# Small experts of an MoE stage in fp32 on two column halves of TensorE, with groups of three kinds

## Chip, core and metric

The kernel runs on one NeuronCore of a Trainium2 chip. The metric is the device time of one execution in microseconds, as the median of several runs.

## What is computed

One inference step of a layer for 1024 prompt rows and 8 streams of 16 rows, 1152 rows of width 2048: a mixer (short convolution and differential attention), then a hierarchical mixture of experts, then a final norm. What matters here is the mixture:

```python
lg = hf @ w_rg + b_rg;  g = argmax(lg)             # 4 groups of experts
le = (hf @ w_re + b_re)[its group];  top 2 of 8    # two experts per row
gu = ragged_dot(xs, w_ei, sizes)                   # 2048 -> 2 x 512, rows sorted by expert
gate, up = split(gu)
ys = ragged_dot(silu(gate) * up, w_eo, sizes)      # 512 -> 2048
y[tok] += ys * weight
```

Everything is fp32. The routing depends on the inputs. Worked out from the reference, the 2304 row-expert pairs of the given inputs fall on the 32 experts in this way:

93, 74, 55, 185, 49, 149, 43, 88, 22, 15, 12, 18, 13, 28, 27, 11, 44, 16, 29, 205, 118, 23, 86, 17, 68, 190, 228, 61, 34, 179, 14, 110.

## The kernel before

Only the expert stage (`phase_experts`) is touched. A group is up to 256 rows of one expert. Every expert here fits in one group, so groups 0 to 31 are the experts in the order above. A group has one tile of 128 rows or two ("a pair", over 128 rows).

**Weights.** An expert's 12.6 MB come as 12 units of 1 MB: 8 units of `w_ei` (256 of 2048 input rows, all 1024 columns) and 4 units of `w_eo` (512 output columns). SP loads them in order into a ring of RAW = 6 buffers (`load_unit`, L1492); it waits on `lo_done` of a buffer before it overwrites it. ScalarE rounds a unit to fp32r in `w_hi` (`split_hi`, L1891), VectorE subtracts to get `w_lo` (`split_lo`, L1979) and thereby frees the raw buffer. `w_hi` and `w_lo` have four slots each; TensorE frees a slot through `used`. So the splits run up to four units ahead of TensorE and the loads six ahead of the splits. The last things ScalarE and VectorE do in a group are the first four splits of the next one.

**Rows.** POOL gathers a group's rows by an indirect DMA per tile (`gather_tile`, L1640), the second tile only for a pair. TensorE transposes them (L1736) a quad of four 128x128 blocks at a time, ScalarE copies a quad to `xT_hi` (L1896) and VectorE makes `xT_lo` (L1984). The first tile of the next group is turned between this group's up and out products. The second tile of a next pair is turned (L1859, L1951, L2140) between `up_and_first` and `out_rest` of this group, under `pe.If(nx < nx2)`; VectorE does this ahead of its last two `split_lo` of the group.

**Products.** Each product is three fp32r matmuls: hi x hi, hi x lo, lo x hi. Up (L1805): 16 blocks of 128 input rows, two halves of 512 columns (256 gate and 256 up), 96 matmuls a tile. Out (L1782): 4 blocks of k, 4 units, 48 matmuls a tile. Between them: silu on ScalarE (L1928), multiply on VectorE (L2117), two transposes a half (L1769), and the hi and lo parts of the activation (L1933, L2122). The two halves let one be activated while TensorE works on the other. ScalarE evicts y (L1965) with the routing weight as scale; POOL scatters the tile's rows to `expert_rows` (L1711).

**Planning.** Ahead of the stage VectorE computes the place of each row, the expert of each group and how many groups before it are pairs. Engines read these as register values (`value_load`, L1564 and L1574). The loop runs 40 times on each engine, with `If(g < count)` around its body, and `by_size` picks a one-tile or two-tile body. POOL writes a table of rows by slot to memory and reads it back into `e_table` (L1691, L1692).

After the last group `phase_final` adds the two expert rows of each token to x and normalizes.

## Time and profile before

| | us |
|---|---|
| median of 3 runs | 3590.74 (3588.39 to 3593.21) |
| the profiled execution, its own time | 3590.53 |
| its span | 3588.5 |
| busy in the span: TensorE matmul / weight load | 3366.8 / 2950.7 |
| busy: VectorE / ScalarE / GpSimd | 1683.9 / 1288.3 / 1021.6 |
| mean granted clock of TensorE | 0.971 of full speed |

All times in the views are microseconds from the start of the span unless marked ns. PE is TensorE's matmuls, PEld its weight loads, DVE VectorE, ACT ScalarE, POOL GpSimd, SP the engine that issues most DMAs. Matmuls are pipelined, so the duration of one is longer than the distance to the next. A true fp32 matmul is listed as two records, an fp32r one as one. "Idle before, releaser" is the engine's idle time ahead of a group of instructions and what ended most of it; "issue" there is time in which it waited for nothing that the profile shows. The granted clock is 1.00 at TensorE's upper level (2.4 GHz) and 0.50 at its lower one (1.2 GHz).

### The profile page before, as it was taken

To read this page: it belongs to the slowest core of one execution; us is meant where nothing else is said; L and a number is where in the kernel's file an instruction comes from. 1 tells how busy PE (TensorE), PEld (TensorE's weight loads), DVE (VectorE), ACT (ScalarE), POOL (GpSimd) and SP (SyncE) were. 2 spreads that over 40 slices of the span, in tenths; PEclk is the share of its full clock that TensorE was granted. 3 is DMA by queue.
4 is the path that set the end of the run, shared out by engine and by line. 5 is a ranking of instruction groups with operands and counts; after the bars stand their busy time and mean duration, and the time that the engine had idled before them with its cause. 6 is when DMAs were issued, how large, how long until landed. Compare 5 with 4: busy or idle time off the path is not lost. (4 is left out here: it accounts for less than half of the span.)

```text
span 3588.5 us, 51245 instructions
## 1 busy us (share of the span) xinstructions
PE 3366.8 (94%) x18439; PEld 2950.7 (82%) x18440; DVE 1683.9 (47%) x1742; ACT 1288.3 (36%) x1577; POOL 1021.6 (28%) x761
## 2 busy tenths in 40 slices
PE   8999999999999998989999869999999999999990
PEld 8999999999999975668888657787888788778770
DVE  4222222000111147860111267658888858846677
ACT  4000000000000035750101246657787757746572
POOL 3444444444444301234445431101111101101010
PEclk9999999999999998999999879999999999999995
DMA  4121111212222391116445469679999979967688
GB/s 150 60 67 54 54 54 58 76 61 75 87 80 67 124 348 61 54 42 238 156 124 164 152 216 356 244 258 354 364 353 369 360 253 369 370 218 268 255 336 361
DMA packets 341083, 691.62 MB, mean 193 GB/s; under 512 B 23034, under 2 KB 151482, under 8 KB 330511
## 3 DMA queue, kind: packets, MB, share of 16 engines
q1 hardware_dynamic: 291508, 585.75, 45.9%
q10 hardware_dynamic: 37163, 66.14, 4.9%
q0 software_dynamic: 12336, 38.69, 3.1%
q8 instruction: 51, 0.84, 0.1%
q14 instruction: 25, 0.20, 0.0%
HBM read 637.25 MB, written 97.28 MB: 205 GB/s over the span
## 5 line engine op out<-in xcount | busy, mean ns | idle before, releaser
L1979 DVE TENSOR_TENSOR e_w_lo<-expert_raw,e_w_hi 128x2048 fp32r<-128x2048 f32 x388 | 872.8, 2288 | 255.1 <-ACT e_w_hi L1891 231.9
L1891 ACT ACTIVATE e_w_hi<-expert_raw 128x2048 fp32r<-128x2048 f32 x388 | 744.3, 1919 | 301.9 <-PE e_gu L1805 253.3
L295 PE MATMUL p_z<-hT_hi,p_w_hi 128*128 128x384 f32 x2256 | 755.3, 335 | 2.4 <-DVE p_xs L432 2.4
L297 PE MATMUL p_z<-hT_hi,p_w_lo 128*128 128x384 f32 x2256 | 753.8, 334 | 0.0
L296 PE MATMUL p_z<-hT_lo,p_w_hi 128*128 128x384 f32 x2256 | 753.7, 334 | 0.0
L295 PEld LDWEIGHTS p_z<-hT_hi,p_w_hi 128*128 128x128 f32 x2256 | 423.6, 188 | 2.7 <-DVE p_xs L432 2.7
L296 PEld LDWEIGHTS p_z<-hT_lo,p_w_hi 128*128 128x128 f32 x2256 | 423.6, 188 | 0.0
L297 PEld LDWEIGHTS p_z<-hT_hi,p_w_lo 128*128 128x128 f32 x2256 | 423.5, 188 | 0.0
L1805 PE MATMUL e_gu<-e_w_hi,e_xT_hi 128*128 128x512 f32 x1216 | 390.4, 392 | 6.6 <-issue 6.6
L1805 PE MATMUL e_gu<-e_w_lo,e_xT_hi 128*128 128x512 f32 x1216 | 387.8, 390 | 0.0
L1805 PE MATMUL e_gu<-e_w_hi,e_xT_lo 128*128 128x512 f32 x1216 | 387.8, 390 | 0.0
L277 POOL TENSOR_TENSOR p_w_raw<-p_w_raw,gain 128x1024 f32<-128x1024 f32 x96 | 182.2, 1898 | 668.8 <-issue 332.6
L1805 PEld LDWEIGHTS e_gu<-e_w_hi,e_xT_hi 128*128 128x128 f32 x1216 | 227.1, 188 | 60.7 <-issue 14.6
L1805 PEld LDWEIGHTS e_gu<-e_w_lo,e_xT_hi 128*128 128x128 f32 x1216 | 228.8, 188 | 48.1
L1805 PEld LDWEIGHTS e_gu<-e_w_hi,e_xT_lo 128*128 128x128 f32 x1216 | 228.8, 188 | 47.9
L1645 POOL COPY e_gather_idx<-e_table 128x2 int32 (+1 forms) x33 | 6.7, 204 | 879.9 <-PE e_t L1736 690.6
L283 POOL TENSOR_TENSOR p_w_lo<-p_w_raw,p_w_hi 128x1024 fp32r<-128x1024 f32 x96 | 237.7, 2476 | 7.7
L626 ACT ACTIVATE d_kT<-p_t 128x512 f32<-128x512 f32 x8 | 4.4, 596 | 613.0 <-DVE p_rows L496 602.3
L1782 PE MATMUL e_y_ps<-e_w_hi,e_aT_hi 128*128 128x512 f32 x608 | 199.9, 410 | 14.8 <-DVE e_w_lo L1979 6.9
L534 ACT ACTIVATE p_e_hi<-p_e 128x1152 fp32r<-128x1152 f32 x8 | 9.3, 1168 | 568.9 <-DVEq L476 568.9
L1429 DVE TENSOR_TENSOR m_x<-m_z,m_x 128x512 f32<-128x512 f32 x36 | 24.6, 692 | 373.1 <-PE m_z L2308 372.7
L1782 PE MATMUL e_y_ps<-e_w_lo,e_aT_hi 128*128 128x512 f32 x608 | 192.6, 398 | 0.0
(337 smaller groups left out, 4642.4 us busy)
## 6 DMA issues: line engine op xcount, KB each, us to landing
expert_raw<-w_ei SPq DMA_DIRECT2D x256, 1024.0 KB, 8.6
expert_raw<-w_eo SPq DMA_DIRECT2D x128, 1024.0 KB, 10.4
p_w_raw<-w_in SPq DMA_DIRECT2D x96, 512.0 KB, 4.0
m_w_raw<-w_out SPq DMA_DIRECT2D x64, 512.0 KB, 4.4
d_k<-cache_k SPq DMA_DIRECT2D x8, 2048.0 KB, 14.6
d_v<-cache_v SPq DMA_DIRECT2D x8, 2048.0 KB, 9.9
rows_back<-expert_rows SPq DMA_DIRECT2D x12, 1024.0 KB, 15.8
n_x<-x SPq DMA_DIRECT2D x9, 1024.0 KB, 5.9
```

Source lines behind the costliest of these rows:

```text
L277: pool.tensor_tensor(w_raw[:, part, :], w_raw[:, part, :], c.gain[:, part].unsqueeze(2).to_broadcast([P, HALF, P]), ALU.mult).then_inc(ste ...
L283: pool.tensor_tensor(w_lo[:, part, :], w_raw[:, part, :], w_hi[:, part, :], ALU.subtract).then_inc(split[half], 1)
L295: pe.matmul(out, w_hi[:, k, :], x_hi[:, xk, cols], start=(k == 0), stop=False)
L296: pe.matmul(out, w_hi[:, k, :], x_lo[:, xk, cols], start=False, stop=False)
L297: mm = pe.matmul(out, w_lo[:, k, :], x_hi[:, xk, cols], start=False, stop=(k == KT - 1))
L534: act.activation(e_hi[:], e[:], ACT.Copy).then_inc(hi_ready, 1)
L1429: dve.tensor_tensor(x[:, s, :], z[:, s, :], x[:, s, :], ALU.add).then_inc(x1_ready, 1)
L1645: pool.tensor_copy(gather_idx[:], field(g, 0)).then_inc(idx_ready, 1)
L1782: mm = pe.matmul(y_ps[:, m % 2, :], a_part[:, r, k, :], w_part[:, s, k * 512:(k + 1) * 512], start=(k == 0 and a_part is aT_hi and w_part ...
L1805: return pe.matmul(gu_ps[:, 2 * r + h, :].rearrange("p (b n) -> p b n", b=2), x_part[:, r, k, :], w[:, :, h, :], start=(k == 0 and x_part ...
L1891: act.activation(w_hi[:, s, :], raw[:, r, :], ACT.Copy).then_inc(hi_done, 1)
L1979: dve.tensor_tensor(w_lo[:, s, :], raw[:, r, :], w_hi[:, s, :], ALU.subtract).then_inc(lo_done[r], 1)
```

## The change

Groups get three kinds, SMALL (at most 64 rows), FULL (up to 128) and PAIR. The planner writes a third table `group_kind`, and each engine branches on it.

A SMALL group multiplies in true fp32 straight from the raw weights: no `split_hi`, no `split_lo`; the raw buffer is freed by the matmul itself. Its rows are held exactly in a new tile `xT` of 64 columns, so a matmul uses half the columns of the array, and the two halves of the output columns run on the two column halves, to PSUM partitions 0 to 63 and 64 to 127. The activation sits on 128 partitions and is done in one piece. Two units of `w_eo` are used at once, which is why they are loaded in the order 0, 2, 1, 3. y lies in halves of 1024 columns on the two partition halves and is scattered as 128 half rows; for this the row table gets two more fields and a copy `twice` doubled over the partition halves.

In other groups the products are as before. The second tile of a pair is now turned at the start of its own group, ahead of the up products, and the first unit is multiplied with the first tile alone before the second tile is awaited. POOL always gathers two tiles. TensorE and ScalarE no longer skip the loop's body behind the last group but branch three times in it.

```diff
+BLOCK_OF = (0, 2, 1, 3)
+FEW = P // 2
+SMALL, FULL, PAIR = 1, 2, 3
+FIELDS = 6
...
-        def by_size(eng, before, after, part):
-
-            with eng.If(before < after):
-                part(2)
-            with eng.If(before == after):
-                part(1)
+        def by_kind(eng, g, part):
+
+            kind = kind_of(eng, g)
+            for k in (SMALL, FULL, PAIR):
+                with eng.If(kind == k):
+                    part(k)
...
-                    gather_tile(0)
-                    with pool.If(before < after):
-                        gather_tile(1)
+                    for r in range(2):
+                        gather_tile(r)
...
+                first_tiles = io.slots.rearrange("(g p) f -> p g f", p=GROUP)[0:FEW, :, :]
+                for h in range(2):
+                    pool.dma_start(twice[h * FEW:(h + 1) * FEW, :, :], first_tiles[:, :, 2:FIELDS]).then_inc(twice_loaded, 16)
...
@@ tensor: up_and_first, start
-                        pe.wait_ge(x_kept, 4 * (g + here + n))
+                        pe.wait_ge(x_kept, 4 * (g + here + 1))
+                        pe.wait_ge(x_exact, 4 * (g + 1))
                         pe.wait_ge(a_kept, 2 * (g + here) + 1)
+                        if n == 2:
+                            turn_second()
...
+                            if u == 0:
+                                for r in range(n):
+                                    if r == 1:
+                                        pe.wait_ge(x_kept, 4 * tile)
+                                    for a in range(2):
+                                        for x_part, w_part in PASSES:
+                                            for h in range(2):
+                                                mm = product(u, a, r, x_part, w_part, h)
...
+                    def up_small():
...
+                        for u in range(UIN):
+                            pe.wait_ge(raw_loaded[u % RAW], 32 * g + 16 * (u // RAW) + 16)
+                            for a in range(2):
+                                k = 2 * u + a
+                                w = raw[:, u % RAW, a * 1024:(a + 1) * 1024].rearrange("p (b h n) -> p b h n", b=2, h=2)
+                                for h in range(2):
+                                    mm = pe.matmul(bank[side(h)], xT[:, k, :], w[:, :, h, :], start=(k == 0), stop=(k == KT - 1))
...
+                            mm.then_inc(lo_done[u % RAW], 1)
+
+                    def turn_act_small():
+                        pe.wait_ge(act_ready, 2 * (g + here) + 2)
+                        for j in range(2):
+                            mm = pe.transpose(gu_ps[:, 0, j * P:(j + 1) * P], act_rows[:, 0, j * P:(j + 1) * P], c.ident[:])
+                        mm.then_inc(a_turned, 2)
+
+                    def out_small(i):
+
+                        units = [UIN + 2 * i + h for h in range(2)]
...
+                        for k in range(KE):
+                            for h, u in enumerate(units):
+                                mm = pe.matmul(y_ps[side(h), i, :], aT[:, k % 2, side(k // 2)], raw[:, u % RAW, k * 512:(k + 1) * 512],
+                                               start=(k == 0), stop=(k == KE - 1))
...
+                    def group(kind):
+                        if kind == SMALL:
+                            up_small()
+                            pe.wait_ge(x_loaded, 32 * (g + 2))
+                            turn_rows(g + 1, g + here + 1, 0, (0,))
+                            turn_act_small()
+                            turn_rows(g + 1, g + here + 1, 0, (1, 2, 3))
+                            for i in range(UOUT // 2):
+                                out_small(i)
+                        else:
+                            up_and_first(tiles_of(kind))
+                            out_rest(tiles_of(kind))
+
+                    by_kind(pe, g, group)
...
@@ scalar
+                    def keep_small(split):
+                        for i in range(UOUT // 2):
+                            for h in range(2):
+                                product_done(UIN + 2 * i + h)
+                            c.hold(act)
+                            act.activation(y[:, 0, i * 512:(i + 1) * 512], y_ps[:, i, :], ACT.Copy,
+                                           scale=column_twice(g, 0)).then_inc(y_kept, 2)
+                            if split:
+                                for h in range(2):
+                                    split_hi(g + 1, 2 * i + h)
+
+                    def group(kind):
+                        n = tiles_of(kind)
+                        if kind == PAIR:
+                            for q in range(4):
+                                act.wait_ge(x_turned, 4 * (g + here + 1) + q + 1)
+                                act.activation(quad(xT_hi, 1, q), second_bank(q).rearrange("p (a b) -> p a b", a=4), ACT.Copy).then_inc(x_hi, 1)
+                        if kind == SMALL:
+                            activate_small()
+                            act.sem_inc(hi_done, UN - AHEAD)
...
@@ vector: keep_rows_lo, and the plan
+                        dve.tensor_copy(xT[:, 4 * q:4 * q + 4, :], bank(t_ps, q % 2)[:, :, 0:FEW]).then_inc(x_exact, 1)
                         dve.tensor_tensor(quad(xT_lo, r, q), bank(t_ps, q % 2), quad(xT_hi, r, q), ALU.subtract).then_inc(x_kept, 1)
...
+                then(dve.tensor_scalar(full_slots[:], group_no[:], 1.0, float(FEW), ALU.min, ALU.mult))
...
+                dve.tensor_reduce(kind_col[:], held[:], AX.X, ALU.add).then_inc(columns_ready, 1)
```

## Rows read from the trace of the kernel before

**Rows 1.** The page's slices: 40 equal parts of the span.

```profile
PE   8999999999999998989999869999999999999990
...
DMA  4121111212222391116445469679999979967688
```

**Rows 2.** Windows by stage: length, busy (count) by engine, clock, DMA share, GB/s.

```profile
2105.00:3496.00 1391.00, 1362.93 (x6232) 1110.22 (x6232) 1020.83 (x686) 950.27 (x839) 180.47 (x147) 0.99 0.85 313
2475.00:2834.00 359.00, 356.84 (x1639) 290.32 (x1639) 311.78 (x201) 284.89 (x240) 47.10 (x41) 1.00 0.97 363
2876.00:2945.00 69.00, 68.69 (x313) 56.37 (x312) 35.84 (x26) 33.00 (x32) 4.61 (x4) 1.00 0.64 234
2834.00:2876.00 42.00, 38.83 (x186) 31.14 (x185) 34.55 (x25) 31.16 (x29) 4.81 (x4) 1.00 0.92 346
2146.00:2182.00 36.00, 35.42 (x164) 28.76 (x162) 30.63 (x21) 28.32 (x24) 6.43 (x5) 1.00 1.01 389
```

**Rows 3.** Lines of the expert stage, by form.

```profile
L1979 DVE TENSOR_TENSOR e_w_lo<-expert_raw,e_w_hi 128x2048 fp32r<-128x2048 f32 x382 | 859.5, 2288 | 255.1 <-ACT e_w_hi L1891 231.9 <-issue 23.0
L1891 ACT ACTIVATE e_w_hi<-expert_raw 128x2048 fp32r<-128x2048 f32 x383 | 735.0, 1919 | 301.8 <-PE e_gu L1805 253.3 <-DMA expert_raw<-w_ei 24.8 <-DMA expert_raw<-w_eo 23.7
L1965 ACT ACTIVATE e_y<-e_y_ps,e_table 128x512 f32<-128x512 f32 x152 | 104.9, 691 | 57.0 <-PE e_y_ps L1782 56.5
L1984 DVE TENSOR_TENSOR e_xT_lo<-e_t,e_xT_hi 128x512 fp32r<-128x512 f32 x128 | 82.4, 686 | 8.9 <-ACT e_xT_hi L1896 7.2
L2122 DVE TENSOR_TENSOR e_aT_lo<-e_gu,e_aT_hi 128x256 fp32r<-128x256 f32 x76 | 31.1, 423 | 35.5 <-ACT e_aT_hi L1933 33.5
L1951 ACT ACTIVATE e_xT_hi<-e_t 128x512 fp32r<-128x512 f32 x12 | 6.5, 595 | 10.9 <-PE e_t L1859 10.9
L1645 POOL COPY e_gather_idx<-e_table 128x2 int32 x32 | 5.9, 185 | 879.9 <-PE e_t L1736 690.6 <-PE e_gu L1859 189.3
```

**Rows 4.** Timeline of TensorE in the up products: start, length, count.

```profile
2852.43 0.62 PE L1805 MATMUL e_gu<-e_w_hi,e_xT_hi 128*128 128x512 f32 x2
...
2852.89 0.61 PE L1805 MATMUL e_gu<-e_w_lo,e_xT_hi 128*128 128x512 f32 x2
```

**Rows 5.** Timeline of TensorE in the decode scores.

```profile
1337.54 1.04 PE L709 MATMUL d_s<-d_kT,d_qx 128*32 128x512 f32 x8
1338.40 0.23 PE L712 MATMUL d_s<-d_kn,d_qx 128*32 128x16 f32 x8
```

**Rows 6.** Timeline of TensorE at the end of group 18, before a pair.

```profile
2856.52 0.60 PE L1736 MATMUL e_t<-ident,e_x 128*128 128x128 f32 x4
...
2858.46 0.44 PE L1769 MATMUL e_gu<-ident,e_act 128*128 128x128 f32 x2 [1.34 <-DVE e_act L2117]
...
2870.05 0.73 PE L1782 MATMUL e_y_ps<-e_w_hi,e_aT_hi 128*128 128x512 f32 x2 [1.44 <-DVE e_w_lo L1979]
```

**Rows 7.** Windows around and behind three waits of TensorE.

```profile
2207.00:2211.00 4.00, 3.69 (x15) 3.15 (x16) 2.35 (x5) 1.45 (x3) 0.00 (x0) 0.61 1.02 409
3187.00:3191.00 4.00, 3.74 (x9) 2.96 (x10) 4.00 (x3) 2.59 (x3) 1.12 (x1) 0.50 0.72 216
2857.00:2860.00 3.00, 1.53 (x10) 1.12 (x9) 1.47 (x5) 2.18 (x6) 0.00 (x0) 1.00 1.02 406
```

**Rows 8.** Waits of TensorE in the stage: us in total, times, longest.

```profile
PE e_gu L1769 <- DVE e_act L2117: 11.0, 9, 2.7
...
PE e_y_ps L1782 <- ACT e_y L1965: 4.8, 6, 3.2
```

**Rows 9.** DMA view: ten groups of one tile; issues of the stage.

```profile
DMA packets 45736, 130.68 MB, mean 363 GB/s; under 512 B 4252, under 2 KB 4252, under 8 KB 45079
...
e_table<-slots POOLq DMA_DIRECT2D x1, 160.0 KB, 13.8
```

**Rows 10.** Timelines of POOL and TensorE at the head of the stage.

```profile
2084.83 2.36 POOL L1640 DMA_INDIRECT e_x<-xg,e_gather_idx  x1 [9.19 <-DVE e_gather_idx L2098]
...
2105.53 1.22 PE L1805 MATMUL e_gu<-e_w_hi,e_xT_hi 128*128 128x512 f32 x2 [6.55 <-issue]
```

More of the change, by code:

```diff
@@ L1641, in gather_tile, with gather @@
                         ap=gather_idx[:, r:r + 1].bitcast(U32), axis=0), bounds_check=TOK - 1, oob_is_err=False).then_inc(x_loaded, 16)
-                def gather(g, before, after):
+                def gather(g):
                     c.hold(pool)
@@ L1679, in _ @@
                 count = group_count(pool)
-                p0, p1, p2 = (pairs(pool, g) for g in range(3))
+                p1 = pairs(pool, 1)
                 pool.wait_ge(x_cleared, 2)
@@ L1683, in _ @@
                 c.hold(pool)
-                gather_tile(0)
-                with pool.If(p0 < p1):
-                    gather_tile(1)
+                for r in range(2):
+                    gather_tile(r)
                 for n in range(LEAD, NP):
@@ L1727, in _, with turn_rows @@
                 pe.sem_inc(y_kept, 2)
-                def turn_rows(tile, r, quads):
+                def turn_rows(g, tile, r, quads):
                     for q in quads:
@@ L1754, in _ @@
                 pe.wait_ge(plan_ready, 1)
-                count, p1 = group_count(pe), pairs(pe, 1)
-                pe.wait_ge(x_loaded, 16 * p1 + 16)
-                turn_rows(0, 0, range(4))
-                with pe.If(p1 > 0):
-                    pe.wait_ge(x_kept, 4)
-                    turn_rows(1, 1, range(4))
+                pe.wait_ge(x_loaded, 32)
+                turn_rows(0, 0, 0, range(4))
                 def body(g):
-                    here, nx, nx2 = (pairs(pe, g + i) for i in range(3))
+                    here = pairs(pe, g)
                     def turn_act(r, h):
@@ L1843, in up_and_first @@
                         turn_act(n - 1, 1)
-                        turn_rows(tile, 0, (2, 3))
+                        turn_rows(g + 1, tile, 0, (2, 3))
                         if n == 2:
@@ L1849, in up_and_first, with turn_second @@
                         out_end(0, n - 1, n, mm)
-                    by_size(pe, here, nx, up_and_first)
-                    with pe.If(nx < nx2):
-                        tile = g + nx + 2
-                        pe.wait_ge(x_kept, 4 * tile)
-                        pe.wait_ge(a_kept, 2 * (g + nx + 1) + 1)
+                    def turn_second():
                         for q in range(4):
@@ L1945, in activate, with keep @@
                         keep_rows_hi(g + here + n, 0, (2, 3))
-                    by_size(act, here, nx, activate)
-                    with act.If(nx < nx2):
-                        for q in range(4):
-                            act.wait_ge(x_turned, 4 * (g + nx + 2) + q + 1)
-                            act.activation(quad(xT_hi, 1, q), second_bank(q).rearrange("p (a b) -> p a b", a=4), ACT.Copy).then_inc(x_hi, 1)
-                    split_hi(g, UN - 1)
-                    act.wait_ge(y_free, g + 1)
-                    c.hold(act)
-                    def keep(n):
+                    def keep(n, split):
                         for b in range(UOUT):
@@ L1974, in _ @@
+                    by_kind(act, g, group)
+                all_groups(act, body)
             @block.vector
```

214 lines of the change are left out of this document (152 added, 62 removed).

## The prediction

> **What bounds the kernel now.** I read the page's slices first [rows 1]: the change touches nothing before 2050 us of the span, and from there to the end of the expert stage near 3496 us TensorE stays at nine tenths while the DMA engines run at six to nine. Then the windows, laid at the boundaries of groups; the mean granted clock of the stage is 0.99 [rows 2]. Ten groups of one tile in a row take 359 us, 35.9 us each, TensorE busy in 356.8 of them, DMA share 0.97. So a lone group is held by TensorE, and the DMA is only 3% behind it. A group of two tiles takes 69 us with the DMA share at 0.64. The stage is thus bound by TensorE, with a second bound close under the small groups. 26 x 35.9 + 6 x 69 make 1347 us, and the stage has 1391 [rows 2]. Of the 44 over it I put 7 on group 0, where everything begins, and 37 on the six pairs, whose second tile is turned ahead of them: the group before one takes 42 us [rows 2].
>
> The routing of the given inputs has 19 experts with at most 64 rows, 7 with 65 to 128, 6 with more (sizes stand above). So 19 groups change kind: 2, 4, 6, the eleven from 8 to 18, 21, 23, 27, 28 and 30. 38 tiles agree with the 152 evictions of y, four to a tile [rows 3].
>
> **Part 1, the small group on TensorE.** Removed: 144 split matmuls at 0.23 us (two start 0.46 us after two [rows 4]), 33 us. Added: 32 fp32 matmuls up and 16 out, each of 512 columns, laid in pairs on the two column halves. The trace has no 64-column case; its nearest row is the decode scores: four fp32 matmuls of 512 columns on four quarters of 32 columns, listed as 8 records, and what follows them begins 0.86 us after them [rows 5]. Alone, one costs as much: a record shows 0.59 us of pipeline, two follow each other, four quarters share them. I take 0.86 us a pair: up 16 x 0.86 = 13.8, out 8 x 0.86 = 6.9. The other end is halves that don't overlap: 27.5 and 13.8.
>
> Between up and out there is a hole. Today the activation reaches TensorE 1.9 us after the last up matmul, and work on the other half hides the rest [rows 6]. In the small group everything waits: 1.9 us, two transposes and the copy to aT (0.42 us and the hand-overs, about 1.2), then VectorE copies and subtracts two quads of the next rows, 2 x (0.42 + 0.64) [rows 3], before the last four transposes, which stand ahead of the out products. I take 6 us (bounds 4 and 8). TensorE does some 1.5 us of transposes in it. Holes of 2.7 and 3.2 us (the longest waits for e_act and for e_y [rows 8]) were each followed by about 4 us with the granted clock near the 1.2 GHz level (0.61, 0.50), one of 1.3 us by none [rows 7]. So the clock falls here and takes 1.7 us from the out products. Sum 28.4 us on TensorE.
>
> Then the hand-over. A group that isn't small needs split weights, and behind a small one no split is ahead: ScalarE turns to them after the first out pair (copy 0.7, hi 1.9, hi 1.9), VectorE follows the first (2.3) [rows 3], and TensorE starts about 1.5 us late: 30 us for a small group that stands alone, 5.9 less than 35.9.
>
> **Part 2, the DMA under it.** Ten groups move 130.7 MB [rows 9], 13.07 MB each. At share 1.01 the engines moved 389 GB/s [rows 2], which makes 33.6 us; I take 34.0 for the eleven in a row (bounds 32.0 at 409 GB/s, which stood for 4 us [rows 7], and 35.9, no gain). The ring of 6 raw units is loaded ahead, 17 us off the front; the last products and the first splits of group 19 add 8. Groups 6 to 18: 30 + 35.9 + (11 x 34 - 17 + 8) = 431 against 467: **36 us** gained. Groups 4, 21, 23, 30 gain 5.9 each, 23.6. Group 2 runs at a full DMA today (its neighbour has share 1.01) and gains 2. Groups 27 and 28 need 18 loads of 2.8 us beyond the ring and 10 behind them, 61 us, gain 10.5. Together **72 us**.
>
> The Trainium skill ("DMA: Bandwidth & Descriptors", Specifications) gives about 358 GB/s as the HBM limit of a core; by that a group would need 36.5 us and the eleven would gain nothing. The trace is against it, with 389 over 36 us.
>
> **Part 3, pairs.** Turning the second tile moves from the end of the group before to the start of the pair. Before, 16 transposes and 1.4 us of wait for a late w_lo [rows 6]. After, the transposes (1.2) and 12 matmuls of the first tile (2.7), then a wait for the second tile's parts: ScalarE first ends its splits, then four quads of 0.55, VectorE its last split and four of 0.65 [rows 3]. Behind a full group or a pair that is about 3.9 us of stall, behind a small one, whose splits are late, 5.5. Each is long enough for the clock to fall, 1.7. So 4 x 8.4 + 2 x 6.8 = 47 against 37: **10 us** lost. The DMA and ScalarE queue behind this stall lose nothing: they are ahead in a pair.
>
> **Part 4, small additions.** The exact copy of each quad (0.42) on VectorE delays the last transposes of 13 larger groups by 0.4: 5. Seven more VectorE steps at 0.2 in the planning chain, before the first rows can be fetched, 1.5; a second gather in front of the first transposes, 1 to 2 (a gather holds POOL for 2.4 there [rows 10]); about 4 in all at the head. The two loads of the doubled table are 5504 pieces of 16 bytes behind the 160 KB table, whose 10240 pieces land 13.8 us after issue [rows 9]; they stand before the gather of group 1: 4 (bounds 0 and 10). ScalarE's extra register load before its evictions is covered by its idle time in front of w_hi; at the end eight empty iterations on TensorE and ScalarE run beside the scatter of the last rows, 2 if that cover is short. Always gathering two tiles costs POOL at most 2.4 us a group [rows 10], hidden in 880 us of its waiting [rows 3]. Sum **15 us**.
>
> **Sum**: -72 + 10 + 15 = -47. The profiled execution took 3590.5 us, the median is 3590.7: **3544 us**.
>
> **Rivals.** (a) *The DMA keeps the long run.* If a group of the eleven can't go under 35.9, 21 us of the gain are gone, and stalls at the hand-overs of twice my size take 12 more: 3577. For it: share 0.97 today. Against: 389 GB/s. The skill's limit above is this case.
>
> (b) *The clock, the other side.* If TensorE stays at 1.2 GHz through the small groups (idle for loads in the up part, then the hole), such a group needs 27.5 + 6 + 13.8 + 1.5 = 49 us, 13 more than today, 19 times 13 plus the 25 of parts 3 and 4: 3863. It turns the sum when a small group passes 34.5 us, that is with more than 12 us of each at the low level. For it: every hole over 2 us lowered the clock [rows 7]. Against: the fall lasted one or two short stretches, and at the low level TensorE has no idle time left in the up part, 3.5 us of work for each 2.8 us load, so it rises again. A milder form, half the groups, gives about 3650. The Trainium skill ("TensorE: Matmul & The Clock Gate", HAM oscillation) describes this case, bursts of products between waits for data that each start at the low clock; by it alone I would forecast slower.
>
> (c) *Code loading.* TensorE's first product waited 6.55 us for nothing that the profile shows, once, when it entered the loop [rows 10], and not again in 31 groups. The loop grows by a quarter. If it no longer stays loaded, each group pays that: 32 x 6.55 - 47 = +163, 3753. It turns the sum at 1.5 us a group.
>
> (d) *The halves don't run together*: 27.5 + 6 + 13.8 = 47 us on TensorE, 3820. Rows 5 speak against it; the change would then not do what it says.
>
> (e) *Cheaper hole and hand-over, faster loads* (4 us, no clock fall, 32.5): 3510.
>
> **How the numbers follow.** Forecast 0.58, (a) 0.14, (b) 0.10, (c) 0.05, (d) 0.03, (e) 0.10. The forecast's own range, from the bounds of the hole, the load rate and the table, is 3520 to 3572. The range to hold 8 in 10 leaves out (b) to (d) beyond mild forms: 3500 to 3600. Faster by over 0.2% (7 us, about what a measurement of this kernel can tell): forecast, (e) and most of (a), 0.75; within it 0.07; slower 0.18.
>
> **What would show it.** Right: in groups 9 to 17 a period of 33 to 35 us with DMA share 1.0 and weight loads as what TensorE waits for; pairs of fp32 matmuls 0.86 us apart; a hole of 5 to 7 us; a stall on e_xT_lo of the second tile after the first 12 matmuls of a pair. Wrong: a period at 36, a granted clock near 0.5 through small groups, or idle time put to issue at every group.

## The result and the profile after

The changed kernel takes 3601.4 us in the median (3595.2 to 3606.4), the kernel before, timed beside it, 3591.8 (3585.2 to 3598.5): ratio 1.0028, 95% interval 1.0019 to 1.0037. It is slower by about 10 us, where 3544 was forecast. The profiled execution has a span of 3593.5 us against 3588.5.

First the slices of the page, which answer to [rows 1]:

```profile
PE   8999999999999998889999758998777799898880
...
PEclk9999999999999999999999879999999999999995
DMA  4121111212222391116445459659999969956788
```

A slice is 90 us. In slices 29 to 32, the run of small groups, TensorE has sunk from nine tenths to seven and the DMA engines stand at nine: there the bound has changed hands. Slice 24, at five where it was at six, is the head of the stage; slice 23, at seven where it was at eight, is the planning ahead of it. The clock's row reads eight and seven there, as it did in the kernel before, so the slices alone say nothing of the clock. The windows (columns as in [rows 2]: length, busy and count of PE, PEld, DVE, ACT, POOL, clock, DMA share, GB/s) are laid on the whole stage, group 0, the run 8 to 18, nine groups of it, the pair behind it, and the full groups 7 and 22, each behind a small one:

```profile
2105.00:3500.00 1395.00, 1190.94 (x5280) 735.62 (x5278) 543.01 (x586) 490.50 (x516) 183.68 (x177) 0.96 0.84 312
2103.00:2159.00 56.00, 39.73 (x164) 31.98 (x164) 31.40 (x25) 28.73 (x24) 26.10 (x18) 0.84 0.69 191
2495.00:2864.00 369.00, 287.32 (x1273) 95.76 (x1272) 57.77 (x134) 49.39 (x80) 35.92 (x52) 0.97 1.01 386
2523.00:2824.00 301.00, 234.15 (x1028) 76.53 (x1026) 45.42 (x108) 37.22 (x63) 30.77 (x45) 0.97 1.02 390
2864.00:2942.00 78.00, 70.39 (x311) 57.33 (x312) 41.63 (x34) 36.85 (x37) 12.64 (x8) 0.96 0.64 235
2452.00:2495.00 43.00, 38.93 (x163) 31.28 (x164) 30.75 (x24) 26.93 (x23) 6.42 (x5) 0.92 0.95 364
3010.00:3050.00 40.00, 37.42 (x164) 29.86 (x163) 30.63 (x23) 26.15 (x23) 6.40 (x5) 0.96 1.00 384
```

Nine small groups take 301 us, 33.4 each, against 35.9 before, at DMA share 1.02 and 390 GB/s. But the pair behind them takes 78 us against 69, group 0 takes 56 against 40, and the full groups 7 and 22 take 43 and 40 against 36, with the DMA at 0.95 and 1.00. Lines of the stage:

```profile
L1994 ACT ACTIVATE e_w_hi<-expert_raw 128x2048 fp32r<-128x2048 f32 x155 | 297.0, 1916 | 247.0 <-PE e_gu L1846 195.9 <-DMA expert_raw<-w_ei 41.1 <-DMA expert_raw<-w_eo 9.5
L1932 PE MATMUL e_gu<-expert_raw,e_xT 128*64 128x512 f32 x1216 | 288.2, 609 | 75.7 <-DMA expert_raw<-w_ei 75.6
```

ScalarE's wait for w_ei in front of a split was 24.8 us in 383 splits and is 41.1 in 155. What TensorE waited for (total, times, longest), answering to [rows 8]:

```profile
PE e_gu L1932 <- DMA expert_raw<-w_ei: 75.6, 79, 4.5
PE e_gu L1846 <- DVE e_xT_lo L2294: 28.7, 5, 7.4
...
PE e_gu L1846 <- DVE e_w_lo L2121: 17.1, 10, 2.9
...
PE e_t L1777 <- DMA e_x<-xg,e_gather_idx: 11.9, 1, 11.9
...
PE e_t L1905 <- issue: 7.8, 1, 7.8
...
PE e_gu L1846 <- issue: 3.9, 1, 3.9
```

**The ledger.** A group's length is from its first up product in the timeline to the next group's. Sums over stretches, in us; the last columns are experiments 4, 3 and 13. Each column is one execution, and that of the changed kernel (3595.2) is the fastest of its eleven, 6 us under its median, so differences of a few us between columns prove nothing by themselves. What lies ahead of the first up product isn't counted. The sums:

```
groups               before   after   none small  run only  best
0, 1                   76.5    94.7      94.8       94.5    87.6
2, 3 (pair)           112.6   109.9     116.1      119.9   103.5
4, 5 (pair)           108.7   112.0     112.4      112.3   107.8
6, 7                   71.7    75.3      72.5       72.5    74.3
8 to 18               400.7   368.6     401.0      368.6   372.4
19 (pair)              69.2    78.6      75.4       78.4    69.6
20 to 23              144.6   138.7     145.9      145.5   139.6
24 to 26 (two pairs)  186.6   196.2     189.5      189.4   194.0
27 to 29 (pair)       148.0   149.7     150.6      152.0   144.2
30, 31                 71.8    72.8      72.6       72.6    72.9
sum                  1390.4  1396.5    1430.8     1405.7  1365.9
```

So nothing is missing from the run of eleven (8 to 18); it is given back in groups 0 and 1, in the pairs, and in the full group behind each small one.

### The profile page after: what moved, and what is told of

Same layout as the page of the kernel before. It is cut to its first block and busy times, and to the rows that moved or that the text cites. A ratio compares the mean times of both kernels' runs of the same rounds, so it can differ in the third digit from the quotient of the medians.

```text
span 3593.5 us, 48571 instructions
## 1 busy us (share of the span) xinstructions
PE 3194.2 (89%) x17491; PEld 2576.9 (72%) x17492; DVE 1209.2 (34%) x1654; ACT 828.8 (23%) x1254; POOL 1025.7 (29%) x796
## 5 line engine op out<-in xcount | busy, mean ns | idle before, releaser
L2121 DVE TENSOR_TENSOR e_w_lo<-expert_raw,e_w_hi 128x2048 fp32r<-128x2048 f32 x160 | 363.9, 2291 | 249.2 <-ACT e_w_hi L1994 247.8
L1994 ACT ACTIVATE e_w_hi<-expert_raw 128x2048 fp32r<-128x2048 f32 x160 | 306.3, 1916 | 247.1 <-PE e_gu L1846 195.9
L1932 PE MATMUL e_gu<-expert_raw,e_xT 128*64 128x512 f32 x1216 | 288.2, 609 | 75.7 <-DMA expert_raw<-w_ei 75.6
L1932 PEld LDWEIGHTS e_gu<-expert_raw,e_xT 128*64 128x64 f32 x1216 | 80.8, 138 | 276.4 <-DMA expert_raw<-w_ei 154.3
L1846 PE MATMUL e_gu<-e_w_hi,e_xT_hi 128*128 128x512 f32 x608 | 203.8, 407 | 51.6 <-DVE e_xT_lo L2294 28.7
L1846 PE MATMUL e_gu<-e_w_lo,e_xT_hi 128*128 128x512 f32 x608 | 200.1, 401 | 0.0
L1846 PE MATMUL e_gu<-e_w_hi,e_xT_lo 128*128 128x512 f32 x608 | 199.6, 400 | 0.0
L1846 PEld LDWEIGHTS e_gu<-e_w_hi,e_xT_hi 128*128 128x128 f32 x608 | 117.9, 197 | 84.2 <-DVE e_xT_lo L2294 30.8
L2471 POOL TENSOR_TENSOR m_w_lo<-m_w_raw,m_w_hi 128x1024 fp32r<-128x1024 f32 x64 | 155.7, 2433 | 5.0
L1954 PE MATMUL e_y_ps<-expert_raw,e_aT 128*64 128x512 f32 x608 | 144.4, 623 | 5.9 <-DMA expert_raw<-w_eo 5.9
```

What stands on the lines that cost most here:

```text
L1846: return pe.matmul(gu_ps[:, 2 * r + h, :].rearrange("p (b n) -> p b n", b=2), x_part[:, r, k, :], w[:, :, h, :], start=(k == 0 and x_part ...
L1932: mm = pe.matmul(bank[side(h)], xT[:, k, :], w[:, :, h, :], start=(k == 0), stop=(k == KT - 1))
L1954: mm = pe.matmul(y_ps[side(h), i, :], aT[:, k % 2, side(k // 2)], raw[:, u % RAW, k * 512:(k + 1) * 512], start=(k == 0), stop=(k == KE - 1))
L1994: act.activation(w_hi[:, s, :], raw[:, r, :], ACT.Copy).then_inc(hi_done, 1)
L2121: dve.tensor_tensor(w_lo[:, s, :], raw[:, r, :], w_hi[:, s, :], ALU.subtract).then_inc(lo_done[r], 1)
L2471: pool.tensor_tensor(self.lo[:, s], self.raw[:, s], self.hi[:, s], ALU.subtract).then_inc(self.split_done, 1)
```

## The experiments

Each starts from the changed kernel, if nothing else is said; the ratio is to the kernel before, run on the same chip. The experiments ran on four chips, on which the kernel before took 3588.4 to 3592.2 us, so the ratios compare better than the times do.

**1. Where the wait at the head comes from.** Behind `pool.wait_ge(slots_stored, ...)` POOL issues the table, the doubled table twice, and then gathers group 1. Its timeline:

```profile
2112.90 3.34 POOL L1720 DMA_DIRECT2D e_table<-slots  x1
2116.22 2.67 POOL L1723 DMA_DIRECT2D e_twice<-slots  x2
...
2121.40 2.60 POOL L1665 DMA_INDIRECT e_x<-xg,e_gather_idx  x1 [1.00 <-POOL e_gather_idx L1670]
```

```diff
                 pool.dma_start(table[:, 6:, :], ...)
-                for h in range(2):
-                    pool.dma_start(twice[...], ...)
                 pool.wait_ge(next_loaded, 16)
                 gather(1)
+                for h in range(2):
+                    pool.dma_start(twice[...], ...)
```

> Edit: the two loads of the doubled table stand behind the gather of group 1's rows on POOL, nothing else. Theory H (the 11.85 us for which TensorE waits in group 0 are these loads in front of the gather): the wait shrinks to under 4 us, group 0 goes from 55.8 to 44-48 us, time 3589 to 3594, that is 7 to 12 us under the changed kernel (3601). Rival R1 (the first groups are short of weights anyway, so what group 0 gives back is asked for again in groups 1 and 2): group 0 is shorter, but group 3 starts at most 3 us earlier, time 3598 to 3602. Rival R2 (the wait is the second gather, not the table): group 0 shorter by under 4 us.

Measured: 3596.6, ratio 1.0016 (1.0005 to 1.0027). TensorE's timeline, the wait for group 1's rows:

```profile
2138.15 1.12 PE L1777 MATMUL e_t<-ident,e_x 128*128 128x128 f32 x4 [8.79 <-DMA e_x<-xg,e_gather_idx]
```

The wait shrank by 3 us only, from 11.85 to 8.79. The doubled table was not the main thing, and H misses. R1 misses by its time, but its sign is there, group 3 starts only 0.7 us earlier (2237.35 against 2238.01); R2's sign is there too, group 0 is shorter by 3.0 us, and the next run tests it. Against the changed kernel's ratio of 1.0028 (1.0019 to 1.0037) no gain in the whole time is certain.

**2. A semaphore for each gathered tile**, on top of edit 1, so that the first doesn't wait for the second.

```diff
-                   ...).then_inc(x_loaded, 16)
+                   ...).then_inc(x_second if r else x_loaded, 16)
-                pe.wait_ge(x_loaded, 32)
+                pe.wait_ge(x_loaded, 16)
```

> Edit: as the run before, and the two gathered tiles count on two semaphores, so that TensorE turns a first tile without waiting for the gather of the second. Theory H with a part for the second gather: 2 to 5 us less than the run before, most of it ahead of group 0 and in group 0 (a gather holds POOL for 2.4 to 2.6 us). Rival (the second gather is hidden everywhere): within 1 us of the run before.

Measured: 3598.5, ratio 1.0022 (1.0012 to 1.0032), not below the run before; the wait for group 1's rows is 9.85 us there. R2 falls: the second gather costs nothing that these runs can tell.

**3. Only the run of eleven small.**

```diff
-                then(dve.tensor_scalar(full_slots[:], group_no[:], 1.0, float(FEW), ALU.min, ALU.mult))
+                then(dve.tensor_scalar(kind_col[:], group_no[:], 7.5, float(FEW), ALU.is_gt, ALU.mult))
+                then(dve.tensor_scalar(full_slots[:], group_no[:], 18.5, None, ALU.is_lt))
+                tt(full_slots[:], full_slots[:], kind_col[:], ALU.mult)
```

> Edit: only groups 8 to 18 may be small (by their number); the eight small groups that stand alone or in twos (2, 4, 6, 21, 23, 27, 28, 30) are multiplied from split weights. Theory L (behind a lone small group the next one is bound by its loads and by splits that come late, and gives back what the small one gained): the time stays within 5 us of the changed kernel or falls, 3585 to 3604, the groups 7, 22, 24 and 31 go back from 43, 40, 46 and 39 us to 36, and groups 4, 6, 21, 23, 27, 30 up to 36-37. Rival (the prediction's sum: lone small groups are worth 5.9 us each, 27 and 28 10.5, less the dearer pairs behind them): 3620 to 3635.

Measured: 3605.8, ratio 1.0040 (1.0027 to 1.0053): 4 us over the changed kernel, which the intervals don't tell apart, and 2 over L's range, far from the rival's. Theory L holds: by the ledger the seven lone small groups from 4 on are worth nothing (groups 4 to 7: 184.8 with full groups, 187.3 with small ones; 20 to 31: 559.5 and 557.4). Groups 2 and 3 are the exception, 119.9 against 109.9. A wait of TensorE for nothing shown stands there in front of the first pair, 5.94 us in this run and 7.79 in the changed kernel; in run 4, whose code for TensorE is the same, it is missing and the two groups take 116.1.

**4. No group small.** Full groups and pairs alone, with all the rest of the change.

```diff
-... group_no[:], 1.0, float(FEW), ALU.min, ALU.mult))
+... group_no[:], 1.0, 0.0, ALU.min, ALU.mult))
```

> Edit: no group is small (the threshold is zero rows), all else as in the changed kernel: what is left is the cost of parts 3 and 4. By the prediction's sum: 25 us over the kernel before, 3616. By the reading of the trace after (head 16 us, exact copies 5, pairs about as dear as before once no small group is ahead of them): 3608 to 3614. Rival (the change's overhead is in the small groups alone): 3591 to 3598. Together with the run before it gives what the run of eleven is worth by itself (28 us by the trace) and what the eight others are worth (theory L: nothing or a loss; the prediction: 34).

Measured: 3631.0, ratio 1.0110 (1.0095 to 1.0125). Neither sum reached that: parts 3 and 4 cost 39 us, not 25. The run 8 to 18, here without small groups:

```profile
2501.00:2902.00 401.00, 397.04 (x1819) 321.03 (x1818) 360.83 (x266) 317.69 (x267) 70.51 (x51) 1.00 0.96 361
```

The run is worth 32 us (401 against 369 in both kernels that have it small), 3 of them returned by the pair behind it.

**5. The gather ahead of the tables.** The DMA view of the changed kernel says why moving the doubled table wasn't enough. In the 12 us in which the rows are awaited:

```profile
q1 hardware_dynamic: 301, 1.15, 92.7%
q0 software_dynamic: 276, 0.25, 12.9%
```

301 weight packets took 92.7% of 16 engines for 12 us, 591 ns each, and brought 1.15 MB. In 12 us of the run of small groups:

```profile
q1 hardware_dynamic: 1896, 4.75, 103.9%
```

4.75 MB, four times as much. But here a packet carries 2.5 KB in the mean, in the 12 us of the wait 3.8 KB, so 591 ns must not be held against the 105 of these. Packets of the larger kind (3.9 KB) ran alone in the kernel before, from 2132 to 2138 us:

```profile
q1 hardware_dynamic: 628, 2.42, 101.0%
```

These took 154 ns each. The tables are pieces of 16 bytes; and before, a packet of such pieces, with no weight load beside it (2114 to 2117 us), took 474 ns (46 packets, 45.4% of 16 engines for 3 us):

```profile
q0 software_dynamic: 46, 0.05, 45.4%
```

So the engines seem to alternate, 301 weight packets to 276 others: a weight packet waits for a table packet. By that estimate it takes 154 + 474 = 628 ns, and 591 were measured. The 276 others are listed with 90 ns each (12.9%), not 474, so the records put the shared time to the weights; in what order an engine served them the view doesn't show. The Trainium skill ("DMA: Bandwidth & Descriptors", Queues, rings and completion order) has this as its rule, an engine goes round the queues by whole packets; the trace agrees, by the counts of 301 and 276 and the sum of 628 against 591 ns. In the kernel before the table began on a DMA without weight loads, the view above lists no other queue. In the same 3 us the changed kernel already loads weights (and issues its table 1.7 us later):

```profile
q1 hardware_dynamic: 476, 0.97, 92.3%
```

```diff
                 pool.dma_start(table[:, 2:6, :], ...).then_inc(next_loaded, 16)
-                pool.dma_start(table[:, 6:, :], ...)     # and the doubled table
                 ...
                 gather(1)
+                pool.dma_start(table[:, 6:, :], ...)     # and the doubled table
```

> Edit: on POOL the gather of group 1's rows goes ahead of the 160 KB table and of the two loads of the doubled table, instead of behind them. Theory H2 (the rows wait behind the table's small pieces, which take turns with the weight loads on the DMA engines; that is why moving the doubled table alone gave only 3 us of the wait back): TensorE's wait for these rows (11.85 us) goes to under 1 us, group 0 takes 42 to 46 us instead of 55.8, group 3 starts at 2224 to 2232 instead of 2238, time 3588 to 3595. Rival R1 (the small pieces cost DMA time that the weights need, wherever they stand): group 3 starts no earlier than 2235, time 3597 to 3603.

Measured: 3593.0, ratio 1.0018 (1.0008 to 1.0028). That is 8 us under the changed kernel's 3601.4, but 3.5 of them are the chip's (3588.4 for the kernel before, against 3591.8). By the ratios some 4 us are left, the intervals overlap, and it is no better than run 1. The wait and the ledger show the effect, the whole time hardly does.

```profile
2128.10 0.66 PE L1777 MATMUL e_t<-ident,e_x 128*128 128x128 f32 x4 [0.58 <-DMA e_x<-xg,e_gather_idx]
...
2150.83 1.22 PE L1846 MATMUL e_gu<-e_w_hi,e_xT_hi 128*128 128x512 f32 x2 [8.21 <-issue]
```

The wait is 0.58 us, as H2 has it, and group 3 starts at 2229: the wait belonged to the table in front of the gather. Group 0 took 48.2 us, though, not 42 to 46, and groups 0 and 1 together 87.3: there is now a wait of 8.21 us for nothing that the profile shows, where the changed kernel has 3.89.

**6. The second tile turned early again.**

```diff
-                        if n == 2:
-                            turn_second()
...
                             turn_rows(g + 1, g + here + 1, 0, (1, 2, 3))
+                            turn_second(1)      # with pe.If(kind_of(pe, g + 1) == PAIR)
...
                             up_and_first(tiles_of(kind))
+                            turn_second(tiles_of(kind))
```

and alike on ScalarE (before the last `split_hi`) and VectorE (before the last two `split_lo`).

> Edit: a pair's second tile is turned at the end of the group before, as in the kernel before (behind a small group: in the hole between its up and its out products). Theory P (turning it at the pair's start costs TensorE 7.4 us behind a small group and 3.6 to 5 behind others, against less at the old place): pairs go from 74-79 to 69-70 us, the group before one gets 3 to 5 us longer, 12 to 25 us less in all, 3577 to 3590. Rival (the stall belongs to the late splits behind a small group, not to the turning): pairs behind small groups stay over 75 us, less than 6 us gained, 3595 to 3602.

Measured: 3588.5, ratio 0.9984 (0.9968 to 1.0000). The twelve runs lie between 3565 and 3593, and the profiled one (3592.5) is the slowest of them, so what follows of the head is the dear case. Groups 4 and 5 together, and the pair alone:

```profile
2322.00:2431.00 109.00, 99.83 (x442) 69.26 (x438) 42.19 (x44) 39.60 (x43) 11.63 (x11) 0.94 0.70 258
2361.00:2431.00 70.00, 68.88 (x312) 56.45 (x312) 32.52 (x28) 29.27 (x30) 7.21 (x5) 1.00 0.64 239
```

Every pair but group 25 is back at 69.6 us, behind small groups too, so the stall belonged to the turning. The groups before a pair pay for it: group 4 took 39.7 against 33.1, its hole 10.7 us. The net is 2.6 us for groups 4 and 5, 5.3 for 8 to 19 (every small group's hole is 0.3 to 0.8 us longer), 5.0 for 27 to 29. And the head got dearer in this execution (groups 0 and 1 took 103 us), by three waits of TensorE:

```profile
2112.13 1.22 PE L1855 MATMUL e_gu<-e_w_hi,e_xT_hi 128*128 128x512 f32 x2 [6.15 <-issue]
...
2170.46 1.21 PE L1855 MATMUL e_gu<-e_w_hi,e_xT_hi 128*128 128x512 f32 x2 [13.36 <-issue]
...
2215.30 5.38 PE L1940 MATMUL e_gu<-expert_raw,e_xT 128*64 128x512 f32 x12 [5.67 <-issue]
```

**7. Two thirds of the bytes.** From group 1 on half of each w_ei load is left out; the products then run on old data, so only the time is read.

```diff
+    if halved and u < UIN:
+        eng.dma_start(raw[:, r, 0:1024]..., w[:, 0:1, :]).then_inc(raw_loaded[r], 16)
+        return
```

> Edit: from group 1 on each load of w_ei brings one of its two halves, so a group moves two thirds of the bytes; the products run as before on whatever lies in the buffers, so the result is not the reference's. Theory L (small groups and the ones behind them are held by the loads): the run of small groups falls from 33.3 to 27.7-28.5 us each, the full groups 7, 22, 24 and 31 from 43, 40, 46 and 39 to 36.3-39, the whole to 3510-3535. Rival (late splits and the clock hold the full group behind a small one): groups 7, 22, 24 and 31 stay within 2 us of what they were.

Measured, in two runs: 3469.3, ratio 0.9672 (0.9655 to 0.9688), far under the expected range. Nine small groups, the full group 22 behind a small one, and pair 5 behind one:

```profile
2509.00:2755.00 246.00, 225.74 (x1030) 82.31 (x1028) 45.91 (x108) 37.19 (x63) 30.79 (x45) 0.94 0.88 324
2925.00:2962.00 37.00, 36.25 (x166) 29.04 (x166) 30.59 (x24) 24.92 (x22) 6.81 (x5) 1.00 0.77 278
2340.00:2418.00 78.00, 71.67 (x322) 58.37 (x320) 35.18 (x32) 31.36 (x35) 12.13 (x9) 0.96 0.41 140
```

A small group takes 27.3 us where loads don't hold it, a full one behind it 36.5 instead of 39 to 43 (group 24, ahead of a pair, 39.4 instead of 45.8). Theory L is shown: both are held by loads, and the rival, by which the full ones would have stayed, falls. The pair stays at 77: its stall is not a matter of loads.

**8. The exact copy only in front of small groups.**

```diff
+                        with dve.If(kind_of(dve, g + 1) == SMALL):
                             keep_rows_lo(g + here + n, 0, (0, 1))
...
+                        with dve.Else():
+                            keep_rows_lo(g + here + n, 0, (0, 1), False)
```

> Edit: VectorE makes the exact copy of the turned rows (0.42 us, four times a group) only where the next group is small. In the run without small groups each full group took 36.2 us, before 35.85. Theory C (the copies cost the larger groups that 0.4 us in front of their last transposes): 11 of the 13 larger groups have a larger or no small neighbour behind only in six cases (0, 19, 24, 25 and the like), so 1 to 3 us gained, 3598 to 3601. Rival (the If's around it cost as much as it saves): no gain, 3601 to 3606.

Measured: 3601.6, ratio 1.0045 (1.0032 to 1.0058): no gain, which is the rival's range. Whether the 0.3 us more of a full group are the copies stays open; there were few places in which this run could show it.

**9. to 11. Both repairs together**, with all small groups, with only the run small, with none (edits 5 and 6 joined, then 3 or 4 added).

> Edit: both repairs at once, the gather of group 1 ahead of the tables and the second tile of a pair turned at the end of the group before; all 19 small groups stay small. Theory A (the two costs are in different places and add up: 8 and 13 us): 3577 to 3584, faster than the kernel before. Rival F (what the gather gives back at the head is asked for again by the first loads of code of the branches, 8.2 us of wait behind group 0 when the gather was early, 13.4 when the second tile was): the same as with the early second tile alone, 3585 to 3592, with a wait of over 10 us for nothing that the profile shows ahead of group 1.

Measured: 3578.7, ratio 0.9957 (0.9944 to 0.9970). It beats both kernels, and yet rival F's sign is there:

```profile
2108.15 1.22 PE L1855 MATMUL e_gu<-e_w_hi,e_xT_hi 128*128 128x512 f32 x2 [6.16 <-issue]
...
2162.24 1.22 PE L1855 MATMUL e_gu<-e_w_hi,e_xT_hi 128*128 128x512 f32 x2 [15.79 <-issue]
...
2207.23 3.68 PE L1940 MATMUL e_gu<-expert_raw,e_xT 128*64 128x512 f32 x8 [6.45 <-issue]
```

22 us of waits for nothing shown, ahead of groups 1 and 2. The DMA view of the longest of them (2146.4 to 2162.3 us) lists packets of a queue of kind instruction:

```profile
q8 instruction: 4, 0.07, 2.3%
```

Nearly all of these waits show the same: of the 31 over 3 us in the expert stages of the sixteen traces, 29 have packets of an instruction queue under way in them, and in the changed kernel none comes between 2236 and 3524 us. Whose code a packet holds the view doesn't say. The five runs of f1 lie between 3569 and 3581, and the profiled one is among the slowest.

> Edit: as f1, and only groups 8 to 18 may be small. Theory L (lone small groups are worth nothing, what they gain the loads take back in the next): within 6 us of f1, either side. Rival (once the pairs behind small groups don't stall, lone small groups pay, some 5 us each): 20 us or more over f1, 3598 to 3612.

Measured: 3580.1, ratio 0.9982 (0.9968 to 0.9995); by the medians within theory L's 6 us of f1. But seven of its twelve runs took 3576 to 3581, five 3592 to 3596, and the ratios lie 9 us apart. Without groups 0 and 1 the profiled executions take 1278.4 us in f1 and 1289.3 here: the lone small groups are worth some 11 us in the repaired kernel, 8 of them in groups 2 and 3. That is more than theory L's nothing and less than the rival's 20.

> Edit: as f1, and no group is small. Theory (the overhead of the change is additive: 39 us in all, of which the two repairs take back 8 and 14): 3603 to 3612; what is left over the kernel before is the exact copies (about 8 us on 26 full groups) and code loaded at first use. The run of eleven small groups is then worth f3 less f2, 28 to 33 us. Rival (the repairs gain only where small groups are): 3620 to 3632.

Measured: 3623.6, ratio 1.0084 (1.0071 to 1.0097). By the median that is the rival's range. But its five runs are two at 3610 and 3612 and three at 3624 and 3625; the profiled one is the lowest, with a wait of 7.25 us ahead of group 0 and one ahead of group 1:

```profile
2156.09 1.21 PE L1855 MATMUL e_gu<-e_w_hi,e_xT_hi 128*128 128x512 f32 x2 [5.39 <-issue]
```

At the lower level the repairs add up as expected, at the upper 13 us are lost again. Something differs from run to run, and it seems to sit at the head: groups 0 and 1 took 81.7 us in this execution at the lower level, and 97.0 in the profiled one of f2, which is at the upper. A profile of one kernel at both levels is missing.

**12. to 14. The order of the branches.** TensorE meets the three branches of `by_kind` one after another in its code. Orders tried: pair, small, full; full, small, pair; and full, pair with the small branch left out and no group small.

```diff
-            for k in (SMALL, FULL, PAIR):
+            for k in (FULL, SMALL, PAIR):
```

> Edit: as f1 (both repairs, all small groups), and on every engine the three branches stand in the order pair, small, full instead of small, full, pair. Theory K (the 15.8 and 6.5 us for which TensorE waits for nothing ahead of groups 1 and 2 are its code at first use: it is thrown off by the jump over the pair's branch): with the full branch last nothing is jumped over behind group 0, that wait falls under 6 us, the time to 3562 to 3572. Rival (the wait goes with the loop's return to its head or with the engine's other loads of code, not with the branch order): 3574 to 3582 as f1.

Measured: 3574.0, ratio 0.9948 (0.9935 to 0.9962), over K's range and not told apart from f1. No wait ahead of groups 1 and 2, as theory K had it; but one of 3.86 ahead of group 4, and one of 10.12 ahead of group 0, which is some 4 more than f1 has there:

```profile
2119.51 1.22 PE L1855 MATMUL e_gu<-e_w_hi,e_xT_hi 128*128 128x512 f32 x2 [10.12 <-issue]
```

> Edit: as f1, branches in the order full, small, pair. Theory K: now two branches are jumped over behind group 0, the wait ahead of group 1 stays at 12 us or more, 3576 to 3590. Rival: as f1, 3574 to 3582, no difference from the order with the full branch last.

Measured: 3568.2, ratio 0.9932 (0.9919 to 0.9946), the best kernel here, 24 us under the one before. Its five runs lie between 3565 and 3570, and f1's lowest (3568.7) is among them. One wait remains, and none ahead of group 0:

```profile
2153.61 1.22 PE L1855 MATMUL e_gu<-e_w_hi,e_xT_hi 128*128 128x512 f32 x2 [9.20 <-issue]
```

> Edit: as f3 (both repairs, no group small), and the code of the small branch left out on every engine, order full, pair. f3 ran at two levels, 3610 to 3612 and 3624 to 3625, its profiled run (the lower) with 5.4 us of wait ahead of group 1. Theory K (the levels are two courses of the code's first loading): less code, all runs at 3604 to 3611, waits for nothing ahead of groups 1 and 2 under 6 us in all. Rival (the levels come from elsewhere): both levels stay, some 13 us apart.

Measured: 3608.0, ratio 1.0047 (1.0034 to 1.0061), all five runs between 3606 and 3612: with less code the upper level didn't appear. One wait, over K's 6 us:

```profile
2150.75 1.22 PE L1855 MATMUL e_gu<-e_w_hi,e_xT_hi 128*128 128x512 f32 x2 [7.03 <-issue]
```

The waits move with the order and number of the branches, but not with them alone. TensorE's code is the same in the changed kernel and in runs 1, 8, 3 and 4, and the wait in front of the first pair is 7.79, 7.70, 4.23 and 5.94 us in the first four and missing in the last. Each stands at a first passage, comes once and goes with instruction packets, so code that is loaded at first use fits all of them; it is argued from that, and no run took the loading away. K had the wrong rule for it: the order with two branches jumped over behind group 0 was the fastest. Whether an order shortens the waits or only makes the short course more frequent stays open, and so does the sequence in which the code comes in.

## Why the prediction was wrong, step by step

**Part 1 held, but for the clock.** A hole of 6 us was forecast. TensorE's timeline of the changed kernel at the end of group 18 and the start of pair 19:

```profile
2849.61 0.44 PE L1942 MATMUL e_gu<-ident,e_act 128*128 128x128 f32 x2 [0.82 <-DVE e_act L2262]
...
2853.15 3.65 PE L1954 MATMUL e_y_ps<-expert_raw,e_aT 128*64 128x512 f32 x16
2857.28 3.65 PE L1954 MATMUL e_y_ps<-expert_raw,e_aT 128*64 128x512 f32 x16 [0.48 <-DMA expert_raw<-w_eo]
2860.87 1.09 PE L1905 MATMUL e_t<-ident,e_x 128*128 128x128 f32 x8
...
2874.17 1.22 PE L1846 MATMUL e_gu<-e_w_hi,e_xT_hi 128*128 128x512 f32 x2 [7.28 <-DVE e_xT_lo L2294]
```

The last up record starts at 2847.6 and the first out pair at 2853.15: 4.9 us of hole. Sixteen records, four pairs, take 3.65 us: 0.86 a pair, as [rows 5] promised; the halves run together, so rival (d) is dead (its price of 3820 comes out at about 3830 by its own terms). The clock fell less often than forecast: of the nine small groups from 2523 to 2824 us, taken one by one, four have it at 1.00 and five at 0.95, the mean is 0.97, and the forecast had it fall in each. So rival (b) did not come true. The Trainium skill ("TensorE: Matmul & The Clock Gate", HAM oscillation) says that in such a kernel each burst of products behind a wait for data starts at the low clock; the trace doesn't agree, with 0.97 in the run, though the waits for loads are short here, 1 us in the mean (75.6 us in 79). Without loads to wait for, a small group took 27.3 us (run 7) against 28.4.

**Part 2 held for the run** (33.4 us against 34.0, DMA share 1.02), and rival (a) falls. The 358 GB/s of the Trainium skill ("DMA: Bandwidth & Descriptors", Specifications) are not this kernel's limit: 390 over 301 us.

**It failed for the lone small groups.** "Groups 4, 21, 23, 30 gain 5.9 each", group 2 gains 2, groups 27 and 28 10.5, and group 6, counted with the run, 5.9 more: 42 in all; by the ledger, after against none small, they gained 5. The step priced the small group by TensorE and left its follower at 35.9. But a small and a full group need 2 x 33.6 = 67 us of loads at 389 GB/s, and their loads didn't reach that rate. Groups 21 and 22, before and after:

```profile
2980.69:3053.05 72.36, 71.59 (x330) 58.10 (x329) 62.44 (x41) 57.00 (x48) 9.06 (x8) 1.00 0.98 373
2978.72:3050.11 71.39, 63.14 (x279) 39.42 (x278) 37.94 (x36) 33.22 (x31) 9.81 (x10) 0.95 0.99 374
```

The two together had 2% of DMA time to give and gained 1 us. Once the small one is cut to 31, the full one finds the ring empty and the splits not done, and waits: 39 to 46 us, against 36 to 41. I had seen the second bound 3% under the first and used it for the eleven, not for the eight. The eleven themselves held: 30 of the 36 forecast for groups 6 to 18 are theirs, and with the pair behind them they gained 29.

**Part 3 was too small.** Ten us forecast, 16 measured without small groups (run 4 against before: groups 2 and 3 +3.5, 4 and 5 +3.7, 18 and 19 +3.8 (group 18 alone 38.7 against 41.1), 24 to 26 +2.9, 28 and 29 +2.1). Behind a small group the stall was given 5.5 and is 7.28, in the last row above. VectorE's timeline shows the queue that was undercounted:

```profile
2861.49 2.29 DVE L2121 TENSOR_TENSOR e_w_lo<-expert_raw,e_w_hi 128x2048 fp32r<-128x2048 f32 x1 [6.58 <-ACT e_w_hi L1994]
...
2869.01 2.35 DVE L2121 TENSOR_TENSOR e_w_lo<-expert_raw,e_w_hi 128x2048 fp32r<-128x2048 f32 x1 [0.18 <-ACT e_w_hi L1994]
2871.63 1.29 DVE L2294 TENSOR_TENSOR e_xT_lo<-e_t,e_xT_hi 128x512 fp32r<-128x512 f32 x2 [0.27 <-ACT e_xT_hi L2086]
2872.84 1.28 DVE L2294 TENSOR_TENSOR e_xT_lo<-e_gu,e_xT_hi 128x512 fp32r<-128x512 f32 x2
```

All four splits of the next group stand ahead of the second tile's quads. What I had as "its last split" is four, because none was made ahead.

**Part 4 failed at the head.** Its terms there were 4 for the chain and gathers, 4 for the tables (bounds 0 and 10). The first of them didn't show: the stage's first product starts at 2103.4 us in the changed kernel and at 2105.5 before. Groups 0 and 1 took 18 us more. Of these 11.85 are the wait for group 1's rows, over the upper bound of 10, and 3.89 the wait that I put to code. The step counted the pieces of the doubled table; runs 1 and 5 show that the table that was there before does it too, once it meets the weight loads. So the price of an unchanged transfer had changed, which no part of the sum asked. The exact copies and the rest, 5 in the forecast, are 6 on the nineteen full groups away from pairs; whether the copies make them stays open by run 8.

**Rival (c)** had the right place and the wrong form: the waits come once, at first passages (3.89 and 7.79 us in the changed kernel, 22 ahead of groups 1 and 2 in f1), not in every group. The kernel before has 6.55 of them, so what the changed one adds is 5.

By the profiles: forecast -47, measured +6 in the stage (+10 in the whole by the medians). Of the 53 between, lone small groups are 37, the run with its pair 1, parts 3 and 4 15. So the step that failed first is the gain of the lone small groups, then the price of the head and of the pairs. The best kernel's stage is 24.5 us shorter than before at this DMA share:

```profile
2105.00:3472.00 1367.00, 1196.07 (x5282) 734.99 (x5282) 543.91 (x586) 490.92 (x516) 177.46 (x178) 0.95 0.85 319
```

## What to carry to other kernels

Where two bounds lie within a few per cent, price a faster step by the sum of both over it and the step behind it: what the buffers can't hold is asked for again. A faster kind pays in full where it stands in a run; alone it was worth 5 us of 42 here, and some 11 by one pair of profiles once the pairs behind it no longer stalled. More room for the loads to run ahead was not tried. When something is added ahead of a small transfer on which the start of a loop waits, look at what else the transfer will meet by then; and count first passages through new branches as a cost of several microseconds, which differs from run to run. Look at all times of a kernel before explaining a difference of ten: the one that is profiled may be its slowest.

## What the runs showed of the hardware

A packet of 16-byte pieces held a DMA engine for 474 ns, and weight packets of 3.8 KB beside such took 591 ns instead of 154; a quarter of the bytes of the run of small groups came in for 12 us. Two fp32 matmuls on the two column halves take 0.86 us together. TensorE's waits for nothing shown, ahead of groups 0 to 4 and each only once, took 4 to 16 us, moved with the order of the branches and also between kernels with the same code for TensorE. With two branches exchanged the median of the whole kernel was 10 us lower (3578.7 and 3568.2, and the first kernel's runs spread over 12 us), and one kernel ran at two levels 13 us apart, of which the upper didn't appear in five runs with a branch left out.
